# Work moved across the phase borders of a two-layer trunk, and the recurrence's key products issued one step ahead

## The reference

```python
xm = rmsnorm(h, norm1) * (1.0 + sc1) + sh1          # sh, sc, g from silu(cond) @ ada_w + ada_b
proj = xm @ w_in                                    # qkv_a, gate_a, a, b, q/k/v_b, u/v_c, q/k/v_d, mgate (4 x 1024)
o_a, s = gdn_mixer(...)                             # gated delta rule, forward and backward
o_b = diff_attention(...); o_c = sgu_mixer(...); o_d = attend(...)
up = einsum('btnw,nwd->btnd', [o_a, o_b, o_c, o_d], w_branch)
merged = sum(sigmoid(mgate) * up)
h = h + g1 * (merged @ w_out)
h = h + g2 * hier_moe(rmsnorm(h, norm2) * (1 + sc2) + sh2)   # 4 groups x 4 experts, 2 chosen per token
```

```python
w = u_i - wk_i @ s
o = qg_i @ s + qk_i @ w
s = exp(gl_i) * s + kd_i^T @ w
```

## Time and profile before

| | us |
|---|---|
| median of three runs (lowest to highest) | 2568.47 (2563.41 to 2570.05) |
| profiled execution, its own time | 2563.89 |
| its span, first to last instruction | 2562.1 |
| TensorE busy | 2276.0 (89%) |
| VectorE busy | 874.8 (34%) |
| ScalarE busy | 551.6 (22%) |
| GpSimd busy | 566.6 (22%) |

### The profile page before, as it was taken

The page is one execution under the profiler, slowest core; times in us unless marked ns, Lnnn a source line. Parts: engine busy times, 40 slices in busy tenths (PEclk is TensorE's granted clock), DMA queues, the critical chain, the costliest instruction groups (busy, mean ns, idle before and its releaser), DMA issues. The chain is left out here.

```text
span 2562.1 us, 32667 instructions
## 1 busy us (share of the span) xinstructions
PE 2276.0 (89%) x12964; PEld 1398.3 (55%) x12964; DVE 874.8 (34%) x1723; ACT 551.6 (22%) x1092; POOL 566.6 (22%) x588
## 2 busy tenths in 40 slices
PE   2999899988999899699959998999889989959993
PEld 1555567765676655233335555777656766533331
DVE  1100555454332335111150017544633424341114
ACT  1000131122333421011130003111243334111112
POOL 0000202315000340555210002032410007025541
PEclk7999989998999999799979999899999999979996
DMA  9341211012111763998764302110211128349865
GB/s 323 130 178 67 55 41 47 31 50 75 40 46 35 267 211 137 371 338 314 249 227 165 133 12 80 46 35 28 68 61 35 49 92 288 118 171 367 323 216 172
DMA packets 181496, 364.60 MB, mean 142 GB/s; under 512 B 54272, under 2 KB 121440, under 8 KB 167648
## 3 DMA queue, kind: packets, MB, share of 16 engines
q1 hardware_dynamic: 135600, 203.04, 22.9%
q0 software_dynamic: 39168, 136.39, 14.1%
q10 hardware_dynamic: 6576, 23.08, 2.6%
HBM read 427.85 MB, written 54.10 MB: 188 GB/s over the span
## 5 line engine op out<-in xcount | busy, mean ns | idle before, releaser
L568 PE MATMUL psum<-arena,h 128*128 128x320 f32 x2048 | 616.4, 448 | 22.6 <-PEq L677 12.7
L568 PEld LDWEIGHTS psum<-arena,h 128*128 128x128 f32 x2048 | 380.0, 194 | 167.7 <-issue 29.4
L407 PE MATMUL psum<-arena 128*128 128x413 f32 (+3 forms) x1184 | 388.4, 489 | 0.0
L407 PEld LDWEIGHTS psum<-arena 128*128 128x128 f32 x1184 | 209.9, 192 | 170.6 <-issue 170.6
L2103 PE MATMUL psum<-arena 128*64 128x512 f32 x1152 | 264.1, 612 | 14.0 <-DMA arena<-in_moe_w,wrow 11.8
L1603 POOL DMA_INDIRECT arena<-in_moe_w,wrow x144 | 143.1, 993 | 249.3 <-issue 135.6
L2103 PEld LDWEIGHTS psum<-arena 128*64 128x64 f32 x1152 | 82.4, 141 | 170.6 <-issue 167.5
L1135 POOL TENSOR_TENSOR arena<-arena 128x644 f32<-128x644 f32 x12 | 23.2, 1934 | 558.7 <-ACT arena L904 558.7
L1458 DVE TENSOR_REDUCE small<-psum 128x1 f32<-128x640 f32 (+1 forms) x120 | 82.2, 712 | 173.9 <-PE psum L1300 173.9
L1720 PE MATMUL psum<-arena 128*128 128x320 f32 x512 | 138.6, 433 | 2.3 <-ACT arena L1809 2.3
L1731 PE MATMUL psum<-arena 128*128 128x512 f32 x320 | 140.5, 594 | 0.0
(11 more groups left out here) (314 smaller groups left out, 2762.1 us busy)
## 6 DMA issues: line engine op xcount, KB each, us to landing
arena<-in_ada_w SPq DMA_DIRECT2D x24, 2048.0 KB, 11.9
h<-in_w_in SPq DMA_DIRECT2D x32, 1024.0 KB, 5.3
gate_rows<-h SPq DMA_DIRECT2D x128, 160.0 KB, 1.8
arena<-gate_rows SPq DMA_DIRECT2D x16, 1280.0 KB, 10.2
y_rows<-arena ACTq DMA_DIRECT2D x72, 256.0 KB, 6.6
arena<-in_w_in SPq DMA_DIRECT2D x8, 1652.0 KB, 7.1
arena<-mod_rows SPq DMA_DIRECT2D x24, 512.0 KB, 7.0
arena<-in_w_branch SPq DMA_DIRECT2D x16, 512.0 KB, 9.4
```

The source lines that it names most:

```text
L407: ins = nc.tensor.matmul(psum[:, 4 + i % 4, 0:w], lhs, rhs, start=(k == 0), stop=(k == KD - 1))
L568: ins = nc.tensor.matmul(psum[:, bank_of(i), 0:HT], gw[c % 2][:, k, f:f + P], gate_xt[:, k, half:half + HT], start=(k == 0), stop=(k == KD ...
```

## The change

- The 64 gate items of a layer are one list with one set of semaphores `W` for both blocks. 271 units are issued in gdn (before: 256, of which 21 behind the last step) and 241 in att. The waits for stores and weight loads at the ends of gdn and att go; the stores are waited for at the start of merge on SyncE.
- More units stand early in gdn (10 instead of 9 items at the start, 3 before the transposes, 2 behind the sums of decays, 12 instead of 8 behind the second set of block products) and in each step (18 instead of 15: two ahead of the query products, three instead of two behind the transposes), with 4 at the end. ScalarE's copies are moved to fit.
- The end of gdn goes: the sigmoid of the gate is ScalarE's first operation of gdn and its product GpSimd's first; square, sum and root of the outputs open att on ScalarE and VectorE; the scaling by tile is put between the attention items (VectorE, after items 10, 14, 18, 22, 26).
- In att, 3 units stand before each of the last five groups of transposes, and where no scores are issued 2 of an item's units are put ahead of the value products. The scaling of the difference heads runs between the last items. Nothing is left behind the last item.
- merge and experts become one block. GpSimd and ScalarE wait on semaphores (`mod_ps`, `row_done`) where the barrier stood, and SyncE clears merge's semaphores later.
- In the recurrence the key products of the next step are issued ahead of the state products of the present one, after `oq`, and VectorE multiplies them by their decays ahead of the state's update.

```diff
-        GCHUNKS = 4 * D // GW // 2
+        GCHUNKS = 4 * D // GW
...
-            FILL_PRE, FILL_KK, FILL_X, FILL_T, FILL_U, FILL_S, FILL_Y = 20, 3, 2, 1, 1, 2, 2
-            FILL_STEP = FILL_KK + FILL_X + len(LEVELS) * (FILL_T + FILL_U) + FILL_S + FILL_Y
+            FILL_PRE = 22 * KD + 1
+            FILL_K, FILL_KK, FILL_X, FILL_T, FILL_U, FILL_S, FILL_Y = 2, 3, 3, 1, 1, 2, 2
+            FILL_STEP = FILL_K + FILL_KK + FILL_X + len(LEVELS) * (FILL_T + FILL_U) + FILL_S + FILL_Y
+            GDN_FILL = FILL_PRE + NT * FILL_STEP + 4
+            GDN_ITEMS = (FILL_PRE + NT * FILL_STEP) // KD
...
-                    gate_moves_done(sp, G, 0)
...
-                    fill(9 * KD)
+                    fill(10 * KD)
...
+                    fill(3)
                     pe.wait_ge(G["qkn"], 4)
...
                     ins.then_inc(G["gcol_ps"], 1)
+                    fill(2)
...
-                        fill((2 - d) * KD)
+                        fill(2 * KD if d == 0 else KD + 4)
                     pe.wait_ge(G["x16"], 2 * (BW - 1))
+
+                    def pair_products(step, first, col, done):
...
+                    pair_products(0, 0, 2, G["kk_ps"])
                     for step in range(NT):
-                        for S_free, first, col in (("s_new", 0, 2), ("o_done", 2, 0)):
-                            if step:
-                                pe.wait_ge(G[S_free], (8 if first == 0 else 2) * step)
-                                pe.wait_ge(G["xt_new"], 2 * nl * step)
...
+                        fill(FILL_K)
+                        if step:
+                            pe.wait_ge(G["o_done"], 2 * step)
+                            pe.wait_ge(G["xt_new"], 2 * nl * step)
+                        pair_products(step, 2, 0, G["kq_ps"])
                         fill(FILL_KK)
...
                         fill(FILL_Y)
+                        if step < NT - 1:
+                            pe.wait_ge(G["oq"], 2 * step + 2)
+                            pair_products(step + 1, 0, 2, G["kk_ps"])
                         for d, t in enumerate(tiles):
                             pe.wait_ge(G["y_done"], 2 * step + d + 1)
...
-                    fill(GITEMS * KD)
+                    fill(4)
...
                         for d, t in enumerate(tiles):
                             egb = bc(eg[:, t, 4 * d:4 * d + 4], [H, DK], 2)
-                            own.link(vec.tensor_tensor(hd(oq[:, d, :]), hd(psum[:, d, 256:512]), egb, ALU.mult))
+                            own.tell(vec.tensor_tensor(hd(oq[:, d, :]), hd(psum[:, d, 256:512]), egb, ALU.mult), G["oq"])
+                        if step < NT - 1:
+                            key_products(step + 1)
...
+            ATT_HEAD = (3 * KD, 3 * KD, 3)
...
-                        fill(KD // 2 if i in (2, 4) else 0)
+                        fill(ATT_HEAD[2] if i else 0)
...
+                        ahead = 2 if i and i + 1 < NI and not scored_with[i + 1] else 0
+                        fill(ahead)
                         if i:
                             values(i - 1)
-                        fill(item_fill[i])
+                        fill(item_fill[i] - ahead)
...
+                        if i % 4 == 2 and 10 <= i < 10 + 4 * NT:
+                            normalize_a((i - 10) // 4)
+                        if i == DIFF_DONE:
+                            square_b()
+                        if i == DIFF_DONE + 2:
+                            v.wait_ge(B["sstd"], 1)
+                            own.link(vec.reciprocal(dss, dss))
+                            normalize_b(0)
+                            normalize_b(1)
+                        if i == DIFF_DONE + 3:
+                            for t in range(2, NT):
+                                normalize_b(t)
...
+            def merge_sync(sp):
+                gates_stored(sp, l, GITEMS)
+                sp.wait_ge(B["ctx_out"], 64)
+                clear(sp, "att")
...
+            def experts_sync(sp):
+                sp.wait_ge(M["stored_mod"], 16 * stored_rows)
+                sp.wait_ge(X["h_ps"], MT - 1)
+                clear(sp, "merge")
...
+                act.wait_ge(M["row_done"], len(modulations))
+                evac_x(0)
...
+                g.wait_ge(M["mod_ps"], 2 * len(modulations))
+                for u in range(2, HU + 2):
```

More of the change, by code:

```diff
@@ L530, in _, with move_gates, gates_stored, gate_filler @@
                 copy_odd(v, own, PN)
[L533 removed]
+        gate_bank = lambda i: 6 + i % 2
+        stores_of = lambda slot, n: len(range(slot, n, 3))
+        def move_gates(sp, l, items):
             for i in items:
                 c, part = i // PER_CHUNK, i % PER_CHUNK
[L537 to L540, removed]
+                if part == PER_CHUNK - 1 and c + 2 < GCHUNKS:
+                    sp.wait_ge(W["gl_ps"], l * GITEMS + i + 1)
+                    load_gate_weights(sp, W[f"gw{c % 2}"], c + 2, l)
+                sp.wait_ge(W["gl_done"], l * GITEMS + i + 1)
                 half = (part % 2) * HT
[L542 to L545 removed]
+                sp.dma_start(gate_rows[c * (GW // P) + part // 2, :, half:half + HT], gout[:, i % 3, :])\
+                  .then_inc(W[f"gs{i % 3}"], 16)
+        def gates_stored(sp, l, n):
             for j in range(3):
[L548 to L555, removed]
+                sp.wait_ge(W[f"gs{j}"], 16 * (l * stores_of(j, GITEMS) + stores_of(j, n)))
+        def gate_filler(pe, l, first):
+            issued = [first]
             def fill(n):
@@ L780, in _ @@
                                 ins.then_inc(G["lb_ps"], 1)
-                        fill((2 - d) * KD)
+                        fill(2 * KD if d == 0 else KD + 4)
                     pe.wait_ge(G["x16"], 2 * (BW - 1))
+                    def pair_products(step, first, col, done):
+                        for d, t in enumerate(tiles_of(step)):
+                            for hh in range(H):
+                                base, c = (hh % 2) * DK, hh // 2
+                                kt = qkv[base:base + DK, 2 + c, pos(t):pos(t) + P]
+                                other = qkv[base:base + DK, col + c, pos(t):pos(t) + P]
+                                ins = nc.tensor.matmul(psum[:, first + hh % 2, (2 * d + c) * P:(2 * d + c + 1) * P],
+                                                       kt, other, start=True, stop=True)
+                        ins.then_inc(done, 1)
+                    pair_products(0, 0, 2, G["kk_ps"])
                     for step in range(NT):
@@ L1063, in _ @@
                             own.send(vec.tensor_tensor(heads(bt[:, d]), prod(0, d), heads(dtm[:, d]), ALU.mult), G["bt"])
+                    key_products(0)
+                    for step in range(NT):
+                        tiles = tiles_of(step)
+                        Xt = Xts[step % 2]
                         v.wait_ge(G["kq_ps"], step + 1)
@@ L1173, in _ @@
                             spread(step + 1)
-                    g.wait_ge(G["o_done"], 2 * NT)
-                    own.tell(nc.gpsimd.tensor_tensor(otmp, o_all[:, :, 0:256], o_all[:, :, 0:256], ALU.mult), G["osum"])
             QK_COLS = T + P
@@ L1406, in _ @@
                     vec = nc.vector
+                    v.wait_ge(B["osq"], 1)
+                    own.tell(vec.tensor_reduce(oss, osq.rearrange("p t (h d) -> p (t h) d", h=H), AX.X, ALU.add), B["oreduced"])
                     v.wait_ge(B["sq"], 1)
@@ new lines, in merge_gpsimd @@
+            def merge_gpsimd(g):
+                own = Own(g, M["own_p"])
+                for i, (n, c, f, half) in enumerate(gparts):
+                    g.wait_ge(M["prod"], i + 1)
+                    dst = mT[:, 4 * c + f, half * HT:(half + 1) * HT]
+                    if n == 0:
+                        own.send(nc.gpsimd.tensor_copy(dst, pr[:, i % 2, 0:HT]), M["sum"])
+                    else:
+                        g.wait_ge(M["sum"], i - PARTS + 1)
+                        own.send(nc.gpsimd.tensor_tensor(dst, dst, pr[:, i % 2, 0:HT], ALU.add), M["sum"])
+                g.wait_ge(M["w_in"], 16 * 9)
+                for st in range(2):
+                    own.send(nc.gpsimd.tensor_tensor(wges[st], wge, bc(scale_f[:, st, :], [KD, 20], 2), ALU.mult),
+                             M["scaled"])
+                for st in range(2):
+                    own.link(nc.gpsimd.tensor_tensor(shifted, wge, bc(shift_f[:, st, :], [KD, 20], 2), ALU.mult))
+                    for w in (4, 2, 1):
+                        out = shift_sum[:, st:st + 1, :] if w == 1 else shifted[:, 0:w, :]
+                        ins = nc.gpsimd.tensor_tensor(out, shifted[:, 0:w, :], shifted[:, w:2 * w, :], ALU.add)
+                        own.link(ins) if w > 1 else own.tell(ins, M["scaled"])
+                g.wait_ge(M["wrow"], 1)
+                load_up(0)
+                load_up(1)
+                g.wait_ge(M["slots"], 1)
+                g.wait_ge(M["mod_ps"], 2)
+                g.wait_ge(M["stored"], 16 * NT)
+                gather(0)
```

(2 more changed lines are left out.)

1283 lines of the change are left out of this document (619 added, 664 removed).

## The result

| | before | after |
|---|---|---|
| median (lowest to highest), us | 2568.39 (2563.41 to 2570.05), 4 runs | 2523.65 (2518.95 to 2527.13), 4 runs |
| profiled execution, its own time | 2563.89 | 2520.91 |
| its span | 2562.1 | 2518.8 |
| TensorE busy | 2276.0 | 2283.4 |
| mean granted clock | 0.949 | 0.947 |

The account below looks back on a forecast made before the run. TensorE, busy 89% of the span, was taken as the bound, with transfers deciding at the experts' start. Terms gave 29.2 us a layer, twice 58.4, plus 7.3 = 65.7, with clock about 68: 2568.5 - 68 = 2500, range 2484 to 2518.

Parts of the forecast that it names:

- gdn ahead of the steps: Before the recurrence, 17 more units fill TensorE's idle time and VectorE loses a small load: 9.75 us a layer.
- the end of gdn: Border to att: VectorE's normalising chain and SyncE's wait for stores leave, 0.7 of 6.3 us idle stays: 5.6 a layer.
- items and end of att: Value products' waits on copied probabilities mostly vanish, 7.06 us a layer; normalising chain and barrier at the end, 5.4.
- the experts: From merge to experts, without the barrier GpSimd starts weight transfers earlier, using idle DMA time: 7.3 us for both layers.
- My new wait of 2.0 lies below the second, so the sum charges nothing.: TensorE's new wait for the last output in each transition, below the harmless 2.41 us, costs no clock.
- The row that I took as proof: Profile row before the change: behind a 2.41 us wait, thirty-two products took 2.06, read as no clock drop.
- The rival that I gave 0.03: Slower: eight waits for `o_done` each drop the clock for the next step, up to 28 us each; chance 0.03.
- The rule of the Trainium skill: Short bursts with waits between can drop the clock every turn; by it each of eight transitions would begin at 1.2 GHz.
- The 1 us of clock a layer: Added gain because the 3.11 us wait ahead of line 717, with slow matmuls behind, and border waits would go.
- The term of the key products: Recurrence transitions: moving key products and decays ahead loses 0.7 us net each, -2.9 for four transitions.
- about 1.8 more for the outputs, as before: In a transition, VectorE's time from updated state to finished outputs, putting `o_done` at about 443.3 instead of 441.5.
- The head of att: Start of att: 15 instead of 8 units, 3 before each group, cover waits of 2.8 and 1.3: 4.1 us a layer.

Follow-up runs that it names:

- experiment 7: The changed kernel with the two units ahead of att's value products put back behind them (`ahead = 0`): 2535.34 us.
- experiment 4: The changed kernel with GpSimd waiting for the last step's outputs before it starts the masks of the next key products: 2507.47 us.
- Experiment 6: The changed kernel with SyncE storing six gate items of att instead of two before it waits for attention's query and key rows: 2513.57 us, again 2515.62.
- Experiment 8: The changed kernel with, first, key products in their old place and six stores ahead: 2482.25 us; second, gap filled, masks late and stores ahead: 2478.44.
- experiment 5: The changed kernel with one of two units ahead of the query products moved behind them: 2531.30 us, beside the changed kernel again, 2522.37.

## Why the prediction was wrong

**The direction and most of the terms were right.** gdn ahead of the steps (19.5 forecast, 19.3 by the stages), the end of gdn (11.6, 14.0), items and end of att (24.9, 24.0) and the experts (7.3, 10.5) came near what was worked out. Only the items have a run of their own (experiment 7); the rest is read from the trace. At the experts the mechanism is not shown: TensorE's wait for the gathered rows, forecast 2 us shorter than 8.1, is 6.0 in the first profile and 8.0 in the second, while the stage gives 10.5 and 10.4.

**The step that failed is the one on the clock: "My new wait of 2.0 lies below the second, so the sum charges nothing."** The wait was 2.42, and behind six of eight such waits the clock fell to its lower level, for 1.5 to 3 us of loss each and 12.3 together. The row that I took as proof, 2.41 us without a drop, is a case that can come out either way: of the eight waits of 2.42, the first of each layer passed undisturbed, and in the second profile of the changed kernel only one did. The rival that I gave 0.03 had the mechanism, and its price of up to 28 us a step was ten times too high, because the clock was back within about 7 us (at most 3 us lost in a step). The rule of the Trainium skill that I set against the row ("TensorE: Matmul & The Clock Gate", section "HAM oscillation - how this bites in real kernels") came out in six of the eight transitions; the trace of before had no transition that could show it. The 1 us of clock a layer that I added had no ground either: it counted the wait of 3.11 ahead of line 717 as gone, and it stayed.

**The term of the key products was mis-sized before the clock comes in.** Forecast -5.8 for eight transitions. With full clock a step takes 33.01 us (444.49 to 477.50), 3.08 more than the 29.93 of before, less 1.64 for three units: a loss of 1.4 instead of 0.7. I had taken "about 1.8 more for the outputs, as before", and it was 2.5 (474.97 to 477.45), since the masks that wait for the decays start sooner as well and hold up one output addition by 0.69 (experiment 4, where the loss is 0.76). TensorE shows only 0.4 of that as a longer wait, as its own two units ended a little later than I had reckoned. I had listed what is queued behind VectorE's moved operation, but not who is released by it. Clock (12.3) and additions (8 x 0.7) make 17.9 of the 18.5 that the recurrence misses.

**The head of att: forecast +8.2, measured -1.6, and +1.7 in the second profile.** I counted 15 units against the waits at lines 1270 and 1275 and these waits did go. What failed is the cover: a unit needs a copied bank, a copy a stored slot, and SyncE's third store stands behind a wait and behind 1 MB of weights. Seven more units in the same stretch run out of slots. Experiment 6 gives some 7 us back, and brings the stage to 7.9.

**The sum.** 18.5 missing in the recurrence and 9.8 at the head of att are 28.3; the other stages gave 4.5 more than forecast, and that leaves the 23.8 between the 65.7 of the forecast by stages and the 41.9 of the table. Experiment 8 closes the account from the other side: with both repaired, the kernel is at 2478 to 2482, 18 to 22 below the forecast. In the trace of the first of the two the head of att gives 8.2, as forecast, and the surplus is in the recurrence (+4.0 where -5.8 was forecast, with the key products in their old place), in the experts (12.0) and at gdn's border (14.0).

Still open is what decides whether a wait of this length halves the clock. Of the eight waits of 2.42 us, the drop came behind 6, 7, 8, 6 and 8 in the five profiles that have them (the changed kernel twice, experiment 6 twice, experiment 7); behind 2.95 (experiment 5) all eight; behind 1.74 (experiment 4) one of eight; behind 1.2 or less in the recurrence none; and behind the 2.41 of before, ahead of the first key products of a layer, none of two.

## What to carry to other kernels

Moving work ahead on an in-order engine delays everything that used to stand before it there, and it also starts its consumers sooner on other engines: list both, and check whether those consumers share a memory port with the delayed work. A filler that is counted in matmuls has a chain behind it (bank, copy, slot, store, queue order); follow that chain before crediting another unit. And a wait in a loop is priced with the clock behind it: compare the same instruction's duration before and behind the wait, and where it is near a level that has halved the clock anywhere, move two or three units into it, which here was worth 30 us and one line. A wait that reads 1.4 us in one layer can be 3.0 in the next: look at both before pricing its removal.

## What the runs showed of the hardware that was not expected

- A VectorE addition with both inputs in SBUF took 1.11 instead of 0.42 us beside GpSimd's masks of 1.25 us each; with the masks moved, all twenty took 0.42.
- Behind equal waits of 2.42 us the granted clock stayed or fell within one execution, and it fell once behind 1.74. Sixteen products took 1.16, 1.66 or 2.08 us right behind it, or 1.17 with the drop only in the units that followed (3.52 for six instead of 1.88).
- Adding a wait to one engine (GpSimd, experiment 4) made the whole kernel some 15 us faster.
